# Sample attention of a two-layer encoder: keys loaded token-minor instead of being transposed on the chip, and their splits moved to the front of the engines' programs

## What is computed

```python
# per running stream: 16 heads, 16 new frames, 1024 past tokens
c_all  = concat([cache_ckv,   c_new])        # (1024 + 16, 256)
kr_all = concat([cache_krope, kr_new])       # (1024 + 16, 64)
s = (einsum('bqhk,bsk->bhqs', q_lat, c_all)
     + einsum('bqhr,bsr->bhqs', q_rope, kr_all)) * ATTN_SCALE
p = softmax(s, axis=-1)                      # no mask: every new frame sees all 1040 tokens
o_lat = einsum('bhqs,bsk->bqhk', p, c_all)
o = einsum('bqhk,khv->bqhv', o_lat, w_uv)
```

## Time and profile before

| | before |
|---|---|
| runs (median of three) | 1939.58 us (1939.31 to 1939.78) |
| profiled execution | 1939.43 us |
| its span | 1937.4 us |
| PE busy | 1905.6 us (98%) |
| PE weight loads | 1801.0 us (93%) |
| DVE busy | 1060.1 us (55%) |
| ACT busy | 766.4 us (40%) |
| POOL busy | 393.4 us (20%) |

### The profile page before, as it was taken

One profiled execution on the slowest core, in us unless ns is written; L12 is line 12 of the kernel. 1 busy time (PEld: TensorE's weight loads), 2 busy tenths in 40 slices (PEclk: granted clock), 3 DMA queues, 4 the chain that ended last, 5 costly groups with the idle time before them and its releaser, 6 DMA issues.

```text
span 1937.4 us, 31334 instructions
## 1 busy us (share of the span) xinstructions
PE 1905.6 (98%) x11703; PEld 1801.0 (93%) x11703; DVE 1060.1 (55%) x1933; ACT 766.4 (40%) x1332; POOL 393.4 (20%) x322
## 2 busy tenths in 40 slices
PE   9999999999999999999999999999999999999998
PEld 8999999999988999999999999999999889988886
DVE  4455445445658512422466666676666677653632
ACT  4333233233412221211455555565555467761100
POOL 0222122122321020000043342432433410000000
PEclk9999999999999999999999999999999999999999
DMA  6122022112236312233201111112011253363421
GB/s 194 33 69 69 22 68 78 43 46 68 93 114 195 125 44 70 80 107 105 93 30 50 43 57 55 37 51 66 28 49 45 71 135 98 96 223 136 158 87 44
DMA packets 159442, 158.54 MB, mean 82 GB/s; under 512 B 36128, under 2 KB 140832, under 8 KB 159104
## 3 DMA queue, kind: packets, MB, share of 16 engines
q1 hardware_dynamic: 153600, 138.81, 23.2%
q10 hardware_dynamic: 5584, 18.16, 2.7%
q0 software_dynamic: 176, 0.43, 0.1%
HBM read 115.52 MB, written 41.84 MB: 81 GB/s over the span
## 4 chain that ended last, share of the span: by engine, by line
PE 54%; DVE 7%; issue 5%; ACT 3%; DMA 1%; DVEq 0%; ACTq 0%; SPq 0%
PE ps L115 16%; PE ps L117 16%; PE ps L116 16%; PE ps L1909 1%; PE ps L1892 1%; PE ps L1891 1%; DVE h_pt_l L109 1%; ACT h_p L2026 1%; DVE h_mx L2152 1%; DVE s_mx L2788 1%; DVE h_p L2109 1%; ACT h_p L2015 1%; DVE h_p L2114 1%; DMA m_g_raw<-scratch_o 0%; DVE h_gate L2174 0%
## 5 line engine op out<-in xcount | busy, mean ns | idle before, releaser
L1805 POOL TENSOR_SCALAR h_p<-h_p,h_rsum 128x128 f32<-128x128 f32 (+7 forms) x128 | 220.7, 1726 | 441.2 <-DVE h_rsum L2156 441.2
L115 PE MATMUL ps<-act_h,a_w_l 128*128 128x384 f32 x768 | 271.4, 353 | 3.4 <-DMA ident<-in_ident 2.8
L117 PE MATMUL ps<-act_h,a_w_h 128*128 128x384 f32 x768 | 261.0, 340 | 0.0
L116 PE MATMUL ps<-act_l,a_w_h 128*128 128x384 f32 x768 | 260.8, 340 | 0.0
L115 PE MATMUL ps<-act_h,m_c_l 128*128 128x384 f32 x480 | 162.9, 339 | 0.0
L117 PE MATMUL ps<-act_h,m_c_h 128*128 128x384 f32 x480 | 162.6, 339 | 0.0
L116 PE MATMUL ps<-act_l,m_c_h 128*128 128x384 f32 x480 | 162.5, 339 | 0.0
L115 PEld LDWEIGHTS ps<-act_h,a_w_l 128*128 128x128 f32 x768 | 145.0, 189 | 8.4 <-issue 3.3
L116 PEld LDWEIGHTS ps<-act_l,a_w_h 128*128 128x128 f32 x768 | 145.2, 189 | 3.3 <-issue 3.3
L117 PEld LDWEIGHTS ps<-act_h,a_w_h 128*128 128x128 f32 x768 | 144.8, 189 | 0.0
L104 ACT ACTIVATE h_pt_h<-ps 128x128 fp32r<-128x128 f32 (+2 forms) x192 | 86.9, 489 | 106.6 <-PE ps L1909 106.5
(11 more groups left out here) (320 smaller groups left out, 4794.2 us busy)
## 6 DMA issues: line engine op xcount, KB each, us to landing
a_w_raw<-in_w_in_a SPq DMA_DIRECT2D x31, 512.0 KB, 3.6
m_c_raw<-in_w_in_b SPq DMA_DIRECT2D x20, 512.0 KB, 4.2
scratch_gate<-m_sg SPq DMA_DIRECT2D x16, 576.0 KB, 5.2
o_w_raw<-in_w_out_b SPq DMA_DIRECT2D x16, 512.0 KB, 6.1
h_gate<-scratch_gate SPq DMA_DIRECT2D x62, 128.0 KB, 2.0
scratch_og<-h_gate SPq DMA_DIRECT2D x62, 128.0 KB, 1.7
o_g_raw<-scratch_og SPq DMA_DIRECT2D x24, 256.0 KB, 4.0
scratch_o<-a_sg SPq DMA_DIRECT2D x8, 576.0 KB, 3.1
```

The source lines that it names most:

```text
L115: nc.tensor.matmul(out, ll, rh, start=first, stop=False)
L116: nc.tensor.matmul(out, lh, rl, start=False, stop=False)
L117: return nc.tensor.matmul(out, lh, rh, start=False, stop=last)
L1805: nc.gpsimd.tensor_scalar(weights_of(u), weights_of(u), rsum[:, u % PB], None, ALU.mult).then_inc(S["p_ready"], 1)
```

## The change

The host hands over the keys a second time, with the token as the last index (`cache_ckv_turned`, `cache_krope_turned`), beside the token-major cache, which the values still need. The kernel loads them so that no key is transposed on PE: all `K` turns go, with `turn_keys` and `turn_first`. `TURNS` is now W0, W1, W4, W2, W3.

The 16 new tokens' columns of all sequences come out of the middle stage: one more latent turn there (three blocks for the tile of the running streams), copied by ACT to a tile `own` of 384 columns and stored to a scratch in memory. Each sequence's load then takes 16 columns of each of three rows of it per partition.

The splits of the keys of sequence `i + 1` become three per period, each 1040 columns wide, from SBUF to SBUF (K0 and K1 the two halves of the latent, K2 the rotary key). On ACT and DVE they stand at the front of period `i`, between the weight turns W1, W4 and W2. The raw keys lie where their low parts will lie (those of sequence 1 in a tile of their own), so that SP loads keys `i` when the scores of sequence `i - 2` are done. The cache splits move behind the weight turns. `normed` is on ACT before and after.

```diff
-TURNS = ["W1", "W4", "W2", "W3", "K0", "K1", "K2", "K3", "K4", "K5", "K6", "W0"]
-BEFORE = TURNS[:4]
+TURNS = ["W0", "W1", "W4", "W2", "W3"]
+BEFORE = TURNS[1:]
...
+    def load_latent_keys(sp, i, par):
+        raw = latent_raw(i, par)
+        sp.dma_start(raw[:, :, 0:PAST], d["cache_ckv_turned"][bass.ds(i, 1)].rearrange("o p a s -> (o p) a s")).then_inc(ct_loaded[par], 16)
+        sp.dma_start(raw[:, :, PAST:KS], own(i)[:, 0:2]).then_inc(ct_loaded[par], 16)
...
         def body(i, par):
 
+            sp.wait_ge(S["s_done"], i * 2 - 2)
+            load_latent_keys(sp, i, par)
+            load_rotary_keys(sp, i, par)
             sp.wait_ge(S["cl_ready"], i * NCP - NCP)
-            load(sp, i, par)
-
+            load_cache(sp, i, par)
...
             scores(i, par, 0, ["W1", "W4", "W2"])
             pe.wait_ge(S["exp_done"], i * 2)
-            scores(i, par, 1, ["W3", "K0", "K1"])
-            values(i - 1, 1 - par, ["K2", "K3", "K4", "K5", "K6", "W0"])
+            scores(i, par, 1, ["W3", None, None])
+            values(i - 1, 1 - par, [None] * 5 + ["W0"])
...
+            if not last:
+                keys_high(act, i + 1, 1 - par, 0)
+            high("W1", i - 1, 1 - par)
+            if not last:
+                keys_high(act, i + 1, 1 - par, 1)
+            high("W4", i - 1, 1 - par)
+            if not last:
+                keys_high(act, i + 1, 1 - par, 2)
+            high("W2", i - 1, 1 - par)
+            exp(i, 0)
+            if not last:
+                q_high(act, i + 1, 1 - par)
+            high("W3", i - 1, 1 - par)
+            normed(i, 0)
             cache_high(act, i, par, 0)
...
+            if not last:
+                keys_low(dve, i + 1, 1 - par, 2)
             largest(i, 0)
-            low("W2", i, par)
+            low("W2", i - 1, 1 - par)
             inverted(i, 0)
...
             if last:
                 k.output.group_low(dve, 0)
+            largest(i, 1)
+            cache_low(dve, i, par, 0)
+            inverted(i, 1)
+            cache_low(dve, i, par, 1)
             cache_low(dve, i, par, 2)
```

More of the change, by code:

```diff
@@ L1051, in middle_programs @@
     kvg = late.take("m_kvg", [KVL])
+    own = late.take("m_own", [3 * P])
     bank = k.bank
@@ L1550, in _ @@
             before, now = behind_gate(j)
-            if before is not None:
+            if before is not None and before < NPB:
                 turned_low_latent(before)
@@ L2314, in samples_programs, with turn_number @@
     names = ("q_loaded uv_loaded zeroed qh_ready ql_ready s_done masked max_done exp_done inv_done p_ready t_done t_high t_out "
-             "o_done o_out ch_ready cl_ready uv_done uv_out og_stored").split()
+             "o_done o_out ch_ready cl_ready kh_ready kl_ready uv_done uv_out og_stored").split()
     S = {n: m.sem("s_" + n) for n in names}
     c_loaded = [m.sem(f"s_c_loaded{i}") for i in range(2)]
[L2318 to L2333, removed]
+    ct_loaded = [m.sem(f"s_ct_loaded{i}") for i in range(2)]
+    kt_loaded = [m.sem(f"s_kt_loaded{i}") for i in range(2)]
+    def turn_number(i, x, par):
+        at = TURNS.index(x)
+        return i * len(TURNS) + at, 6 + (par + at) % 2
     def seqs(eng, body):
@@ L2430, in turn_bank @@
         return bank[:, at]
[L2432 to L2456, removed]
     @block.tensor
@@ L2473, in turn @@
         def turn(x, i, par):
[L2475 to L2487, removed]
+            n, at = turn_number(i, x, par)
+            turn_weights(int(x[1]), i, n, at)
         def scores(i, par, qt, beside):
@@ L2530, in body @@
                     heads.bank_free(pe, b)
[L2531 to L2544, removed]
+                pe.wait_ge(S["zeroed"], 6)
+                for qt in range(2):
+                    scores(i, par, qt, [None] * 3)
+                turn("W0", i, par)
                 return
+            if isinstance(i, int) and i == 1:
+                pe.wait_ge(S["zeroed"], 12)
+            pe.wait_ge(S["exp_done"], i * 2 - 1)
             scores(i, par, 0, ["W1", "W4", "W2"])
             pe.wait_ge(S["exp_done"], i * 2)
-            scores(i, par, 1, ["W3", "K0", "K1"])
-            values(i - 1, 1 - par, ["K2", "K3", "K4", "K5", "K6", "W0"])
+            scores(i, par, 1, ["W3", None, None])
+            values(i - 1, 1 - par, [None] * 5 + ["W0"])
         seqs(pe, body)
-        turn("W1", NSEQ, 0)
+        turn("W1", NSEQ - 1, 1)
         k.output.first_columns(pe, 0)
         for x in ("W4", "W2", "W3"):
-            turn(x, NSEQ, 0)
+            turn(x, NSEQ - 1, 1)
         k.output.first_columns(pe, 1)
         pe.wait_ge(S["o_out"], NSEQ - 1)
-        values(NSEQ - 1, 1, None)
+        values(NSEQ - 1, 1, [None] * 6)
     def project_values(pe, j):
@@ L2588, in q_high, with keys_part, keys_high @@
         nc.scalar.activation(rq[0:RD, par].rearrange("p (h l) -> p h l", h=HEADS), qr_raw[0:RD, :, cols], ACT.Identity, scale=SCALE).then_inc(S["qh_ready"], 1)
[L2590 to L2600, removed]
+    def keys_part(i, par, j):
+        if j == 2:
+            return kt_raw[par][:, 0:KS], kt_h[par][:, 0:KS], kt_l[par][:, 0:KS]
+        return latent_raw(i, par)[:, j], ct_h[par][:, j, 0:KS], ct_l[par][:, j, 0:KS]
+    def keys_high(act, i, par, j):
+        if j == 0:
+            act.wait_ge(ct_loaded[par], (i - par) * 16 + 32)
+            if not (isinstance(i, int) and i < 2):
+                act.wait_ge(S["s_done"], i * 2 - 2)
+            if isinstance(i, int) and i == 1:
+                act.wait_ge(heads.S["pv_done"], PAIRS * NG)
+        elif j == 2:
+            act.wait_ge(kt_loaded[par], (i - par) * 24 + 48)
+        raw, high, _ = keys_part(i, par, j)
+        round_high(nc, high, raw).then_inc(S["kh_ready"], 1)
     def cache_high(act, i, par, n):
@@ L2763, in low @@
         def low(x, i, par):
-            if isinstance(i, int) and i < NSEQ and x not in turns(i):
-                return
-            n, at = turn_number(i, x)
+            n, at = turn_number(i, x, par)
             j = int(x[1])
-            if x[0] == "K":
-                return keys_low(dve, j, n, at, 1 - par)
             b = bank[:, at]
@@ L2832, in body @@
                 k.output.row_low(dve, 0)
-            for x in ("K6", "W0"):
-                low(x, i, par)
+            low("W0", i, par)
         seqs(dve, body)
         for x in BEFORE:
-            low(x, NSEQ, 0)
+            low(x, NSEQ - 1, 1)
     def gate_values(dve):
```

165 lines of the change are left out of this document (67 added, 98 removed).

## The result

The changed kernel takes **1943.94 us** (median of 20 runs, 1941.66 to 1945.73) against 1939.76 for the kernel before: a ratio of 1.0021, 95% interval 1.0015 to 1.0027. It is slower by 0.2% where 0.3% faster was forecast, and above the range given. The profiled execution takes 1944.91 us, 5.5 more than the one of before.

What follows compares the result with a forecast made beforehand. PE set the pace before; after the change a serial ACT and DVE chain would bind the steady periods. Terms -6.7 - 1.65 + 3.8 - 1.3 + 0.35 = -5.5 gave 1934.1 us, range 1930.5 to 1939.5.

Steps and rivals of the forecast that it cites:

- the clock's term: PE behind the new stalls: the clock was taken to stay at its upper level, so nothing was added to the sum.
- the new stalls: PE waits 2.1 us ahead of the values in each steady period, and 3.9 ahead of the first output columns.
- the rival that had it: PE's clock halves behind the stalls, so values take 6.5 us more, five times: 1967 us; chance 0.04.
- Steady periods: Sequences 2 to 6: each falls from 19.65 to 18.3 us, five times 1.35 less, -6.7.
- The chain: ACT and DVE splits, maximum, exponential, W3 in series: the values start 11.36 us into a period, PE free at 9.3.
- Sequences 0 and 1: Together 31.35 us against 33.00, -1.65, with sequence 1 waiting for the keys of sequence 2, landing 6 after issue.
- The 64 B runs: Load of the 16 new columns: priced at nothing beyond issue; the skill's rule would add 1 us once, 1935.1.
- The slower rival of late keys: Latent loads follow each other, landing 11.5 us after issue, delaying sequence 1 and steady periods: 1943.9 us; chance 0.10.
- Last sequence: DVE splits the gate group ahead of tile 1's maximum; output columns start 20.43 in instead of 16.61, +3.8.
- Heads' last pair and middle stage: Before the sequences: key turns gone from the heads' last pair, -1.3 (0 to 4.1 saved); one more middle-stage turn, +0.35.
- Full gain: PE stays the bound over the sequences, a period 16.68 us, all eight sets of turns come back: 1916; chance 0.04.

Runs made afterwards that it cites:

- E2: The changed kernel with the low part of the rotary keys (K2) moved on DVE behind the maximum and W3's low part: 1932.08 us.
- E4: The changed kernel with ACT and DVE in another order, the next keys' splits spread over the period behind maximum and exponential: 1918.33 us.
- E1: The changed kernel with unused identity transposes on PE, ahead of the last score chunk of sequences 1 to 6 and the first output columns: 1937.41 us.
- E3: The kernel before, with only the last sequence's first gate group split on DVE ahead of query tile 1's maximum: 1944.36 us.

## Why the prediction was wrong

**The step that failed** is the clock's term: the sum put the cost of PE's clock behind the new stalls at nothing, and the rival that had it got 4%. The reason given was one row, a stretch in which PE was busy for 1.26 of 3.00 us and the clock stayed at 1.00. But behind four of six stalls of some 2 us, and in the gap of 3.58, the clock fell.

That row was one draw. It holds a wait of 2.78 us, and E2, whose program is the same there, waits 2.81 at that place. The waits before and in E2, and the windows behind them in the same order (the clock stands third from the end):

```profile
8.74 0.69 PE L115 MATMUL ps<-act_h,a_w_l 128*128 128x384 f32 x1 [2.78 <-DMA ident<-in_ident]
8.77 0.44 PE L115 MATMUL ps<-act_h,a_w_l 128*128 128x384 f32 x1 [2.81 <-DMA ident<-in_ident]
...
10.00:13.00 3.00, 3.00 (x11) 3.00 (x10) 2.52 (x3) 2.99 (x4) 0.00 (x0) 1.00 1.08 382
10.00:13.00 3.00, 3.00 (x11) 2.76 (x10) 2.53 (x4) 2.95 (x4) 0.00 (x0) 0.50 1.08 385
```

Of the nine profiled executions of this document the clock stays at 1.00 over 7 to 13 us in two, before and E4 (waits of 2.78 and 2.69), and falls in seven (waits of 2.81 to 3.92). So one execution in which a gap cost nothing did not clear the gaps to come. At the start the fall is harmless: the product that begins at 22.78 before begins at 22.82 after the change.

The Trainium skill ("TensorE: Matmul & The Clock Gate", Why this matters for your kernels) advises against idle gaps between bursts of matmuls, and names gaps longer than the stalls of some 2 us. The gap of 3.58 agrees with it; the falls behind stalls of 2.10 to 2.46 go beyond it, and there the measurement decides.

The rival's price was off as well, in the other direction. The prediction took all 6.5 us of values at half speed, 6.5 more each time; the clock came back in between, and a fall behind a stall cost 8.06 - 6.56 = 1.5. The sequences with the output's first part take 164.93 (1569.01 to 1733.94) against 156.99 in E1, so that the clock cost 7.9 there.

**The terms of the sum, without the clock**, from E1 and the profiled executions:
- *Steady periods:* 18.50 against 18.3, -5.7 instead of -6.7. The chain holds link by link; its hand-overs add 0.24.
- *Sequences 0 and 1:* 31.53 against 31.35, -1.5 instead of -1.65. K0 of sequence 2 waits for its load as forecast. Timeline of ACT after the change:

```profile
1583.48 1.07 ACT L104 ACTIVATE s_ct_h<-s_ct_raw 128x1040 fp32r<-128x1040 f32 x1 [1.97 <-DMA s_ct_raw<-scratch_own]
```

SP issues the big load at 1577.10 and the small one 1.13 later, and the wait for both ends 6.4 after the first issue (6 forecast).
- *The 64 B runs:* the load of the own columns lands as long after its issue as the big one:

```profile
s_ct_raw<-in_cache_ckv_turned SPq DMA_DIRECT2D x7, 1024.0 KB, 5.2
...
s_ct_raw<-scratch_own SPq DMA_DIRECT2D x7, 16.0 KB, 5.2
```

The rule of the Trainium skill on transfers under 512 B ("DMA: Bandwidth & Descriptors", Specifications) shows no cost of its own in these rows. The slower rival of late keys did not happen either, since the landing of 6.4 is far from the 11.4 that it needed; that its 1943.9 is the time that came is chance.
- *Last sequence:* the first output columns start 20.42 in, 20.43 forecast; 32.94 to the main part against 32.8, +3.9.
- *Heads' last pair and middle stage:* E4, in which the clock does not fall, takes 38.19 from the wait for `h_gate` at 1529.82 to sequence 0, against 38.81 before: -0.6, where -1.3 was taken between 0 and -4.1, so that this term had half its size. In the profiled execution after the change the clock fell there too, and it is 39.05. The middle stage's turn is +0.3 (+0.35); by the `h_gate` wait at the head of that pair the executions after the change and of E4 are 0.65 and 0.51 behind the one of before (1529.96 and 1529.82 against 1529.31); the rest of that is spread over the stages ahead and is in no term.

That makes -5.7 - 1.5 + 3.9 - 0.6 + 0.3 = -3.6 where -5.5 stood, and E1 confirms the size: 2.6 below the kernel before, with the fall in the heads still in it. With about 8.8 for the clock (7.9 and 0.9 in the heads) the change comes to +5.2, against 5.5 between the profiled executions (4.2 between the medians).

**Full gain.** It was dismissed at 4%, and for the order as changed that was right: the serial chain binds, not the average. E4 shows that a time near the 1916 of that rival was within reach of the same instructions in another order (1918). Its period is 16.15 where the rival had 16.68, so the turns' price of 2.97 was low by 0.5: part of the 19.65 of before were short waits, 0.32 of the 20.00 us in the earlier trace rows.

## What to carry to other kernels

Where PE is the bound and its work is cut, walk the other engines' new order link by link, and put what the next engine waits for (here the maximum) ahead of work for the next period; moving one split of 1.2 us was worth 12, half of it because the clock then held. Price a new stall of PE not only by its own length but with the chance of a slow stretch behind it, even where an earlier gap did no harm in one trace: 2 us of waiting cost up to 1.5 more. A wait that can't be removed can be bridged by idle products, as E1 shows, but finding the order without the wait was worth four times as much.

## What the runs showed of the hardware

- PE's granted clock fell to 0.50 behind four of the six stalls of 1.85 to 2.46 us in one execution, and stayed at 1.00 behind the other two (2.15 and 1.85). Stalls of 1.03 to 1.46 in E2 left it at 1.00. With the waits of 3.58 (the change), 3.57 (E2) and 2.46 (E3) ahead of the output's first columns it fell each time. What decides between stalls of one length stays open; no run was made for it.
- At the kernel's start, in code that no run changes, the clock fell in seven of nine profiled executions and stayed at 1.00 in two, with waits of 2.78 (kept) and 2.81 (fell) nearest to each other.
- Idle transposes kept the clock: with the stalls filled by them it was 1.00 over the sequences in E1, where without them it fell.
- In the heads' last pair the same code with waits of 1.76 and 1.94 kept the clock at 1.00 in E4's profiled execution and lost it in those of the change and of E1 (0.66 over 1557 to 1562). Whether this makes the spread of the changed kernel's runs, 4.1 us, is not shown: of the twenty, the three with a mean clock of 0.994 take 1941.97 to 1942.52, but 0.993 stands beside both 1941.66 and 1945.73.
